# Hybrid decoder layer on one core: where the next stage's first weight pieces are cast, the mixed stream split and the residual loaded

## What is computed

```python
h = rmsnorm(x)                                   # project_ssd
z, xbc, dt = h @ w_in[...]; xbc = silu(dwconv(xbc))   # project_ssd
y, h_last = ssd_scan(x, dt, a, b, c, h0)         # scan
o_ssd = rmsnorm(y * silu(z)) @ w_ssd_o           # merge_ssd
q, k, v = h @ w_in[...]                          # project_nsa
kc, vc = compress(k), compress(v)                # compress_rows
o_nsa = nsa_attend(q, kc, vc, k, v) @ w_nsa_o    # attend_prompt, merge_nsa
o_mem = softmax(q_mem @ mem_k.T) @ mem_v @ w_mem_o     # project_mem, memory_branch
mixed = sum(sigmoid(gate_i) * o_i)               # in the three merges
x = x + mixed @ w_out                            # finish_layer
u = dwconv(rmsnorm(x) @ w_up)                    # finish_layer
x = x + (silu(u[:2816]) * u[2816:]) @ w_down     # finish_layer
```

## Time and profile before

| | us |
|---|---|
| median of three runs | 1811.5 |
| lowest and highest of them | 1809.32, 1811.58 |
| the profiled execution | 1811.66 |
| span of the profiled execution, first to last instruction | 1809.5 |
| PE busy in it | 1669.5 (92%) |
| DVE busy | 955.7 (53%) |
| ACT busy | 704.0 (39%) |
| POOL busy | 698.5 (39%) |

### The profile page before, as it was taken

How to read it: one execution, slowest core, us unless ns; L and a number is a source line. 1 busy time by engine, 2 the same in 40 slices (tenths; PEclk the granted TensorE clock), 3 DMA queues, 4 the chain that set the end, 5 groups by cost and what they waited for, 6 DMA issues and landing times. The chain is left out here.

```text
span 1809.5 us, 33710 instructions
## 1 busy us (share of the span) xinstructions
PE 1669.5 (92%) x13060; PEld 1517.4 (84%) x13060; DVE 955.7 (53%) x1525; ACT 704.0 (39%) x1402; POOL 698.5 (39%) x362
## 2 busy tenths in 40 slices
PE   6999996886998999879998999989989799999999
PEld 5999995555998999536666898978789799999999
DVE  4477666996511452247775255542224488888200
ACT  3333335784511331135554333333323344444211
POOL 2344445994344333124444340012143244444443
PEclk8999998998999999879999999989999899999999
DMA  4222225543222432214002324435424122222233
GB/s 146 72 81 93 93 81 185 187 173 111 77 93 77 147 105 100 98 50 161 1 0 72 140 94 150 177 108 230 152 70 146 65 93 87 87 92 93 85 89 120
DMA packets 60396, 193.64 MB, mean 107 GB/s; under 512 B 6964, under 2 KB 19764, under 8 KB 56756
## 3 DMA queue, kind: packets, MB, share of 16 engines
q1 hardware_dynamic: 58996, 190.30, 31.1%
q10 hardware_dynamic: 1312, 2.14, 0.3%
HBM read 174.47 MB, written 22.14 MB: 109 GB/s over the span
## 5 line engine op out<-in xcount | busy, mean ns | idle before, releaser
L264 POOL TENSOR_TENSOR mm_ring<-mm_raw,mm_ring 128x1024 fp32r<-128x1024 f32 x154 | 378.6, 2460 | 737.1 <-ACT mm_ring L241 594.3
L241 ACT CAST mm_ring<-mm_raw 128x1024 fp32r<-128x1024 f32 x160 | 167.6, 1048 | 491.9 <-PE up_pp L274 225.5
L274 PE MATMUL up_pp<-h,mm_ring 128*128 128x260 f32 x2016 | 244.4, 284 | 6.3 <-POOL mm_ring L264 6.3
L274 PEld LDWEIGHTS up_pp<-h,mm_ring 128*128 128x128 f32 x2016 | 244.3, 190 | 6.7 <-issue 6.7
L274 PE MATMUL ssd_pp<-h,ssd_ring 128*128 128x260 f32 x1920 | 235.5, 286 | 3.0 <-POOL ssd_ring L264 3.0
L274 PEld LDWEIGHTS ssd_pp<-h,ssd_ring 128*128 128x128 f32 x1920 | 234.9, 191 | 3.2 <-ACT gates_raw L525 3.2
L264 POOL TENSOR_TENSOR ssd_ring<-mixed,ssd_ring 128x1024 fp32r<-128x1024 f32 x42 | 102.3, 2437 | 170.8 <-ACT ssd_ring L241 153.9
L274 PE MATMUL up_pp<-act_t,mm_ring 128*128 128x260 f32 x1344 | 162.1, 282 | 5.8 <-POOL mm_ring L264 5.8
L274 PEld LDWEIGHTS up_pp<-act_t,mm_ring 128*128 128x128 f32 x1344 | 161.6, 188 | 6.2 <-issue 6.2
L274 PE MATMUL nq_pp<-h,mm_ring 128*128 128x260 f32 x960 | 121.7, 288 | 5.9 <-DVE nq_t L1362 5.9
L274 PEld LDWEIGHTS nq_pp<-h,mm_ring 128*128 128x128 f32 x960 | 118.6, 191 | 6.9 <-DVE nq_t L1362 6.1
(11 more groups left out here) (416 smaller groups left out, 2867.0 us busy)
## 6 DMA issues: line engine op xcount, KB each, us to landing
mm_raw<-in_w_up SPq DMA_DIRECT2D x44, 512.0 KB, 3.6
mixed<-in_w_ssd SPq DMA_DIRECT2D x42, 512.0 KB, 3.4
mem_ring<-in_mem_kv SPq DMA_DIRECT2D x16, 1024.0 KB, 6.0
mm_raw<-in_w_ssd_merge SPq DMA_DIRECT2D x24, 512.0 KB, 3.5
mm_raw<-in_w_mkv_qm SPq DMA_DIRECT2D x24, 512.0 KB, 3.6
mm_raw<-in_w_qk SPq DMA_DIRECT2D x20, 512.0 KB, 3.5
sc_seg<-cum_rows SPq DMA_DIRECT2D x16, 512.0 KB, 5.1
mixed<-in_ssd_state SPq DMA_DIRECT2D x16, 512.0 KB, 3.9
```

Source lines behind the costliest of these rows:

```text
L241: act.copy(self.ring[:, b % 2, 0], self.raw[:, b % 2]).then_inc(self.high, 1)
L264: pool.tensor_tensor(self.ring[:, u, 1], self.raw[:, u], self.ring[:, u, 0].bitcast(F32), ALU.subtract).then_inc(self.low, 1)
L274: last = pe.matmul(out(n), self.ring[:, b % 2, wn, k], x[:, xn, chunk + k, part], start=start and k == 0 and wn + xn == 0, stop=stop and k ...
```

## The change

Nine edits in seven functions. (1) The last stores of `project_ssd` are no longer waited for there but in `scan`, and their two buffers lie in the weights' raw slots. (2) In `scan` the first pieces of the merge are loaded from step 12 on, cast by ACT behind steps 14 and 15, and subtracted by POOL in step 14 and step 15, ahead of the last gate. (3) `merge_ssd` multiplies with `r` ahead of the evacuation. (4) The first retirement of semaphores is gone. (5) `project_nsa` clears one element instead of a tile, and ACT issues the last two stores. (6) `attend_prompt` waits for its constants one score later. (7) `memory_branch` runs its merge unrolled and splits chunk after chunk of `mixed` on ACT and DVE beside it, all but the last. (8) `finish_layer` splits the last chunk only, loads `x` in three parts between the pieces of `w_out`, and multiplies `w_out`'s first tiles in turn. (9) `w_up`'s first two pieces are multiplied in turn, the last chunk of the first waiting for the norm's last chunk; ACT casts piece 2 before Ln and piece 3 where it cast both.

```diff
@@ multiply: parameter last_chunk=None
+            if last_chunk is not None and k == size - 1:
+                pe.wait_ge(*last_chunk)
@@ project_ssd, SP
             sp.dma_start(d["out_s_conv"], conv_s[:]).then_inc(stored, 16)
-            sp.wait_ge(stored, 32)
@@ scan, SP, in step v
+                if v + AHEAD == STEPS:
+                    sp.wait_ge(conv_stored, 32)
+                    for b in range(2):
+                        following.load_piece(sp, 0, b)
...
-            for b in range(2):
-                following.load_piece(sp, 0, b)
@@ scan, POOL, in step v
                 if v + 1 < STEPS:
                     mix(v + 1)
+                else:
+                    following.write_low_of(pool, 0, 1)
+                if v + 2 == STEPS:
+                    pool.wait_ge(mixed_up, STEPS)
+                    following.write_low_of(pool, 0, 0)
...
-            pool.wait_ge(mixed_up, STEPS)
-            for b in range(2):
-                following.write_low_of(pool, 0, b)
             gate(STEPS - 1)
@@ scan, ACT, in step v
-            for b in range(2):
-                act.wait_ge(mixed_up, STEPS - AHEAD + 2 * b + 1)
-                following.write_high(act, 0, b)
+                if v + 2 >= STEPS:
+                    b = v + 2 - STEPS
+                    act.wait_ge(mixed_up, STEPS - AHEAD + 2 * b + 1)
+                    following.write_high(act, 0, b)
@@ merge_ssd, DVE
+                    m = at(mixed, t)
+                    dve.tensor_tensor(m, m, r[:], ALU.mult).then_inc(weighed, 1)
                     w.finished(dve, i * 2 + (GATES + u), 1)
-                    m = at(mixed, t)
+                    dve.wait_ge(weighed, t + 1)
                     dve.tensor_tensor(halves(m), po[:, u, :, 0:HALF], halves(m), ALU.mult).then_inc(evacuated, 1)
-                    dve.wait_ge(evacuated, t + 3)
-                    dve.tensor_tensor(m, m, r[:], ALU.mult)
@@ build_layer, after merge_ssd
-        Stage.hold(w_qk.semaphores)
-        Stage.retire_semaphores(nc)
@@ project_nsa, SP to ACT, and DVE
-            sp.wait_ge(evacuated, 2 + w.tiles)
-            sp.dma_start(d["out_cmp"], qk[:, CK:CK + 4, :]).then_inc(stored, 16)
-            sp.dma_start(d["out_v"], vt[:]).then_inc(stored, 16)
+            act.wait_ge(evacuated, 2 + w.tiles)
+            act.dma_start(d["out_cmp"], qk[:, CK:CK + 4, :]).then_inc(stored, 16)
+            act.dma_start(d["out_v"], vt[:]).then_inc(stored, 16)
-            dve.memset(t2[:], 0.0).then_inc(evacuated, 2)
+            dve.memset(t2[0:1, 0:1], 0.0).then_inc(evacuated, 2)
@@ attend_prompt, PE
-            pe.wait_ge(walled, 2)
             for j in range(NJ):
+                if j == 1:
+                    pe.wait_ge(walled, 2)
                 score(0, 0, j, first=True)
@@ memory_branch, ACT
+            def take_mixed(t):
+                act.wait_ge(evacuated, t + 3)
+                act.copy(mixed_split[:, 0, t, :], mixed[:, t, :]).then_inc(mixed_high, 1)
+            for t in range(KC):
+                w.write_ahead(act, KC // 2 + t // 2, t % 2, t // 2 == KC // 2 - 1)
+                if t:
+                    take_mixed(t - 1)
             following.write_first_after(act, w)
@@ memory_branch, DVE, after the add of tile t
+                if t:
+                    dve.wait_ge(mixed_high, t)
+                    dve.tensor_tensor(mixed_split[:, 1, t - 1, :], mixed[:, t - 1, :],
+                                      mixed_split[:, 0, t - 1, :].bitcast(F32), ALU.subtract).then_inc(mixed_low, 1)
@@ finish_layer, SP; PARTS = ((0, 2), (2, 5), (5, KC))
-            sp.wait_ge(src_low, KC)
-            sp.dma_start(x[:], d["x"]).then_inc(loaded, 16)
-            w_out.load(sp)
+            for t in range(2, KC):
+                sp.wait_ge(w_out.low, t - 1)
+                w_out.load_piece(sp, t // 2, t % 2)
+                if t - 2 < len(PARTS):
+                    a, b = PARTS[t - 2]
+                    if b == KC:
+                        sp.wait_ge(src_low, 1)
+                    sp.dma_start(x[:, a:b, :], d["x"][:, a:b, :]).then_inc(loaded[t - 2], 16)
@@ finish_layer, PE
-            w_out.multiply_pair(pe, lambda b, n: po[:, b, n, 0:HALF], split, HALF_PARTS, src_low)
-            for t in range(2, KC):
-                pe.wait_ge(added, t - 1)
-                w_out.multiply(pe, t // 2, t % 2, lambda n: po[:, t % 2, n, 0:HALF], split, 0, HALF_PARTS)
+            for t in range(KC):
+                if t >= 2:
+                    pe.wait_ge(added, t - 1)
+                w_out.multiply(pe, t // 2, t % 2, lambda n: po[:, t % 2, n, 0:HALF], split, 0, HALF_PARTS,
+                               last_chunk=(src_low, 1) if t == 0 else None)
             pe.wait_ge(evacuated, 1)
+            pe.wait_ge(added, KC - 1)
+            pe.wait_ge(low, KC - 1)
+            w_up.multiply(pe, 0, 0, lambda n: pp[:, 0, 0, n, 0:HALF], h, 0, HALF_PARTS, last_chunk=(low, KC))
             pe.wait_ge(added, KC)
-            w_up.multiply_pair(pe, lambda b, n: pp[:, 0, b, n, 0:HALF], h, HALF_PARTS, low)
+            w_up.multiply(pe, 0, 1, lambda n: pp[:, 0, 1, n, 0:HALF], h, 0, HALF_PARTS)
@@ finish_layer, ACT
-            high_of(act, x, split, KC, src_high)
+            act.copy(split[:, 0, KC - 1, :], x[:, KC - 1, :]).then_inc(src_high, 1)
...
             square(KC - 1)
+            w_up.write_high(act, 0, 2)
             act.wait_ge(summed, 1)
...
-                    w_up.write_ahead(act, i, u, last)
+                    if first and u == 0:
+                        w_up.write_high(act, 0, 3)
+                    else:
+                        w_up.write_ahead(act, i, u, last)
```

More of the change, by code:

```diff
@@ L265, in write_low_of, with multiply @@
                            ALU.subtract).then_inc(self.low, 1)
-    def multiply(self, pe, i, b, out, x, chunk, parts, start=True, stop=True):
+    def multiply(self, pe, i, b, out, x, chunk, parts, start=True, stop=True, last_chunk=None):
         pe.wait_ge(self.low, i * (2 * self.per) + (b + 1))
@@ L443, in project_ssd @@
         r = s.sb("nx_r", [P, COLS])
+        assert nc.sbuf_base <= end, (nc.sbuf_base, end)
         PIECES = 4
@@ L625, in _ @@
                 o.leave(rounds)
+    return stored
 LOG1P_TERMS = 7
@@ L2523, in project_mem, with memory_branch @@
         following.begun = True
-def memory_branch(nc, d, c, h, om, both, mk, mv, qm, mixed, w, ring, landed, following, gate, spare):
+def memory_branch(nc, d, c, h, om, both, mk, mv, qm, mixed, mixed_split, w, ring, landed, following, gate, spare):
     KB = MEM // P
@@ L2816, in _, with finish_layer @@
             dve.wait_ge(gated, KC)
[L2817 to L2826 removed]
+            for t in range(KC):
+                first = (6, 0)[t % 2]
+                w.finished(dve, KC // 2 + t // 2, t % 2)
+                g = gate[:, t, :]
+                o(dve.tensor_tensor(halves(g), banks[:, first:first + 2, 0:HALF], halves(g), ALU.mult))
+                o.settle()
+                dve.tensor_tensor(mixed[:, t, :], mixed[:, t, :], g, ALU.add).then_inc(evacuated, 1)
+                if t:
+                    dve.wait_ge(mixed_high, t)
+                    dve.tensor_tensor(mixed_split[:, 1, t - 1, :], mixed[:, t - 1, :],
+                                      mixed_split[:, 0, t - 1, :].bitcast(F32), ALU.subtract).then_inc(mixed_low, 1)
         following.begun = True
[L2831 removed]
+def finish_layer(nc, d, c, h, x, split, act_t, w_out, w_up, w_down, spare, end):
     with ExitStack() as ctx:
         s = Stage(nc, ctx)
[L2838 removed]
+        PARTS = ((0, 2), (2, 5), (5, KC))
         sq = spare[:, 0:2]
         acc = spare[:, 4:8].rearrange("p (a b) n -> p a b n", a=2)
+        sil = s.sb("up_sil", [P, 2, COLS])
         sq_sum = s.sb("nf_sq_sum", [P, COLS])
@@ L2850, in finish_layer @@
         po, pd, total = pp[:, 0], pp[:, 0], pp[:, 1, 1]
-        src_high, src_low, loaded, added = (s.sem("po_" + v) for v in ("src_high", "src_low", "loaded", "added"))
+        src_high, src_low, added = (s.sem("po_" + v) for v in ("src_high", "src_low", "added"))
+        loaded = [s.sem(f"po_loaded{n}") for n in range(len(PARTS))]
         squared, gathered, summed, logged, scaled, high, low = (s.sem("nf_" + v) for v in (
@@ L3025, in _ @@
                 w_out.finished(dve, t // 2, t % 2)
+                for n, (a, b) in enumerate(PARTS):
+                    if t == a:
+                        dve.wait_ge(loaded[n], 16)
                 dve.tensor_tensor(halves(x[:, t, :]), po[:, t % 2, :, 0:HALF], halves(x[:, t, :]), ALU.add).then_inc(
@@ L3150, in build_layer @@
                 xbct = s.sb("xbct", [P, XBC, COLS])
+                raw_at = ring_at + 4 * chunk
+                tails = s.over("ssd_tails", [P, XBC, CONV - 1], F32, raw_at)
+                conv_s = s.over("ssd_conv_s", [P, XBC, DEC, CONV], F32, raw_at + chunk)
                 dt_at = s.here()
@@ L3215, in build_layer @@
                 assert nc.sbuf_base <= ring_at, (nc.sbuf_base, ring_at)
```

(5 more changed lines are left out.)

43 lines of the change are left out of this document (13 added, 30 removed).

## The result

| us | before | changed |
|---|---|---|
| median of the runs | 1811.54 (1809.32 to 1812.81) | 1786.73 (1785.42 to 1790.43) |
| profiled execution | 1811.66 | 1786.26 |
| its span | 1809.5 | 1784.4 |
| mean granted clock of PE | 0.958 | 0.965 |

The ratio is 0.9866, interval 0.9849 to 0.9883: 24 to 25 us less, in the range and 2 us from the 1785 forecast. A second set of runs of the changed kernel gave 1785.59 (1781.79 to 1790.93).

The account below looks back on a forecast made before the run. PE, busy for 92% of the span, was taken as the bound, with savings at the seams between stages. Seven terms, 1.5 + 4.6 + 1.5 + 2.5 + 1.0 + 4.3 + 11.0 = 26.4, off 1811.66 gave 1785 us, range 1777 to 1799.

Parts of the forecast that it names:

- End of project_ssd, 1.5: Seam into scan: without the wait for the store the scan begins earlier; 1.5 us, from 0.8 to 1.75.
- End of scan, 4.6: Scan into merge_ssd: earlier casts and subtractions leave SP's state store last; 4.6 us gained, from 2.6 to 5.7.
- merge_ssd to project_nsa, 1.5: PE starts right behind POOL without barrier and memset; 1.5 us gained, from 0.4 to 2.0.
- moving it frees nothing by itself: End of merge_ssd: DVE's last scaling ended ahead of POOL, so moving it gains nothing alone.
- compress_rows, 2.5: Start of compress_rows: with the stores on ACT's queue the small table lands 2.5 us earlier, from 0 to 4.5.
- rival (a): compress_rows: the queues are no queues, the table lands as late, nothing gained there; 1787.8 us; chance 0.14.
- attend_prompt, 1.0: Start of attend_prompt: scores needing no constants start earlier, behind POOL's first copy; 1.0 us gained, from 0 to 1.9.
- rival (d): attend_prompt: the lower clock holds on after the moved start, costing 48 us over 134 us; 1833 us; chance 0.04.
- memory_branch to finish_layer, 4.3: Splits beside the merge and w_out's earlier piece 2 let tile 2 start in time; 4.3 us gained, 3.0 to 6.4.
- w_up's first tiles, 11.0: Start of w_up: pieces in turn, with piece 2 covering the wait behind the norm's sum; 11.0 us gained.
- without gaps pieces 0 and 1 end at T + 13.3: w_up: piece 0 starts at T + 1.7, both pieces end at T + 13.3, the norm's sum at T + 14.4.
- The lower bound of 6: w_up: gain of 6 us if the first piece falls to half clock and piece 3's wait isn't covered.

Follow-up runs that it names:

- the other two traces with the wait: Second trace of the unchanged kernel before (1814.82 us), and changed kernel with project_ssd's store wait, first retirement, full memset and attend_prompt's early constants wait restored (1793.69 us).
- the second trace of before: The kernel before, profiled once more with nothing changed: 1814.82 us.
- 5.3 by the experiment: Changed kernel with mixed split at finish_layer's start, x loaded at once and w_out's first tiles paired again: 1791.31 us, ratio to before 0.9888.
- 9.2 by the experiment: Changed kernel with w_up's first two tiles as a pair again and the casts of pieces 2 and 3 behind the norm's scale: 1797.73 us, ratio to before 0.9912.

## Point by point: where the prediction held

1. **End of project_ssd, 1.5:** 1.86 at the seam. In the profiled pair 1.4 of it is left at the scan's first gate and 0.9 at its first state update, which comes 28.91 us behind ACT's last SiLU in before and 27.97 in the changed kernel. The pair is not the rule: 32.24 and 31.70 in the other two traces with the wait, 27.97 to 28.51 in all ten without, so up to there the edit is worth 0.4 to 4.3 us. Why it spreads so is not shown. The size at the seam is right. (A further 1.1 us of that stretch was gained ahead of any edit's place, in the first tiles, where the clock from 40 to 44 us stood at 0.57 in both traces of before and at 1.00 in the changed kernel; in three variants it stood at 0.57 too, so this is no effect of the edit.)
2. **End of scan, 4.6:** 4.9 from the state update to the matmul, 3.9 for the stage in the pair (6.9 against the second trace of before). The mechanism is as put down: SP's store last, landing 4.2 behind its issue where 3.9 was taken, 4.8 from issue to matmul where 4.3 was taken, DVE's update waiting for POOL's scaling (0.60). Behind it some of it goes back: merge_ssd starts at half clock as before, and for longer (its first 26 matmuls take 5.3 us where they took 4.5).
3. **merge_ssd to project_nsa, 1.5:** 1.94. The failed detail is "moving it frees nothing by itself": POOL's last subtraction, begun at 581.73 beside DVE's scaling, which ran to 582.17, took 2.63; with no DVE instruction beside it it takes 2.34. Barrier and memset are 1.66 of the 1.8 forecast, the larger second retirement costs 0.1, not 0.3 (1.47 from DVE's last instruction ahead of it to the next issue, 1.36 before; this lies at attend_prompt's start).
4. **compress_rows, 2.5:** 0.09. This term failed, and rival (a) had it right. The step that failed is the reading of the small store on ACT's queue as evidence that a separate queue helps: in the changed kernel it stood behind the two stores on its own queue and cm_pos on an empty one, and both landed when the stores did (ACT's idle 6.61, DVE's 4.46). The rows of before already had a part of the answer: the small store (gates_turn) was issued 1.5 us behind cm_pos, so that much of its shorter time is its later issue (rows behind this list). The bound "0, if it lands as before" was in the range.
5. **attend_prompt, 1.0:** 1.08 at the seam, and 0.8 to 2.2 more behind it, where the clock doesn't fall a second time. The second part wasn't foreseen; rival (d) had looked at that same stretch and feared the opposite.
6. **memory_branch to finish_layer, 4.3:** 5.0 in the pair, 5.3 by the experiment. DVE's last subtraction ends 0.56 behind POOL's (0.6 forecast), tile 2 has no gap. The two first tiles took 13.3 us (ACT's next cast is at 1356.25) instead of the 13.8 put in.
7. **w_up's first tiles, 11.0:** 8.95 in the pair, 9.2 by the experiment, 10.5 in traces in which the clock stays up. With T = 1392.73 - 1.97 = 1390.76, the end of w_out, the steps are: piece 0 at T + 1.97 (T + 1.7 forecast), the sum's start at T + 15.1 (T + 13.3), a gap of 0.62 ahead of piece 3 (0.5), its end at T + 28.6 (T + 26.5). The mis-sized step is "without gaps pieces 0 and 1 end at T + 13.3": the clock fell in piece 0. The lower bound of 6 had that case, together with a wait of piece 3 that did not come.

The small store in the order of instructions of before (cm_pos is issued at 726.70; ACT's next issue follows the landing of gates_turn):

```profile
725.87 0.43 SPq L1309 DMA_DIRECT2D out_v<-vt  x1
...
728.24 0.54 ACTq L1531 DMA_DIRECT2D gates_turn<-tr_gs  x1
...
733.42 0.34 ACTq L1533 DMA_DIRECT2D gates_s<-gates_turn  x1
```

The windows of w_up's first pieces (us; PE busy and count; granted clock; DMA share; GB/s), of the changed kernel and of the one with the stores behind the loads, from w_up's first matmul:

```profile
1392.73:1398.73 6.00, 6.00 (x37) 0.72 0.53 178
...
1398.73:1405.73 7.00, 7.00 (x60) 1.00 0.07 22
```

```profile
1389.04:1395.04 6.00, 6.00 (x50) 1.00 0.54 175
...
1395.04:1402.04 7.00, 7.00 (x57) 1.00 0.25 71
```

The idle time ahead is the same, 1.97 and 1.96 us, and so is the work. In one the clock falls and 37 matmuls pass in the first 6 us, in the other 50.

**The sum.** 26.4 was forecast, 25.4 measured between the profiled executions (25.14 in the table). Set against the table, four stretches gave less than forecast: compress_rows up to its first matmul with cm_w (0.09 for 2.5) 2.4, its rest with attend_prompt's start (-0.47 for 1.0; +0.67 against the second trace of before) 1.5, w_up (8.95 for 11.0) 2.05, the end from w_up on (-1.34 for nothing) 1.3; 7.3 together. Five gave more: project_mem 3.2, attend_prompt behind its start 0.8, memory_branch to finish_layer 0.7, project_ssd with the scan 0.7 (6.81 for 6.1), merge_ssd with project_nsa's start 0.6; 6.0 together. So the mechanism was right for six of seven terms, one of them (w_up) with a size too large, but the nearness to 1785 is partly chance: effects that the prediction did not contain, of about the size of its errors, with the other sign.

## What to carry to other kernels

Here a small table landed only behind the stores that were given to the DMA engines before it, on whichever of the two queues they stood: order the loads that the next stage waits for ahead of stores that nobody waits for (here 6 to 8 us by the medians, 5.8 of it found in the traces, for issuing two stores behind four loads). Sum a change up seam by seam and check each seam in the trace, cut at the same instructions, since a total near the forecast can hide terms that failed. And where runs of one kernel differ by 5 us, take a second trace of the kernel before, to see which stages move by themselves.
